# A two-layer hybrid decoder step on one core: split-weight ring restarted, first four output chunks of two stages done row by row, embedding gate moved to VectorE

## The reference

```python
for i in range(2):
    z = rmsnorm(h, norm1[i]) @ w_in[i]              # 2560 columns: pooling input, q, k, v, gate
    h = h + concat(pool(z), retention(z)) @ w_o[i]
    hn = rmsnorm(h, norm2[i])
    if i == 0:  f = (silu(hn @ wg) * (hn @ wu)) @ wd           # dense, D_FF = 2816
    else:       f = sum over 8 experts of gate_e * swiglu_e(hn)    # top 2 of 8, 1408 wide
    h = h + f
    gate = sigmoid(h @ w_ple_gate[i])
    h = h + gate * (p[i] @ w_ple[i])                # the embedding gate
y = rmsnorm(h, final_norm)
```

## Time and profile before

| | |
|---|---|
| median of three runs | 984.67 us |
| the profiled execution, its whole time | 982.37 us |
| its span, first to last instruction | 980.6 us |
| mean granted TensorE clock | 0.972 |
| TensorE busy | 925.4 us (94%) |
| VectorE busy | 718.1 us (73%) |
| ScalarE busy | 523.2 us (53%) |
| GpSimd busy | 141.7 us (14%) |
| share of the chain that ended last | PE 86%, DVE 5%, ACT 4%, issue 2%, POOL 2% |

### The profile page before, as it was taken

One profiled execution on the slowest core, in us unless ns is written; L12 is line 12 of the kernel. 1 busy time (PEld: TensorE's weight loads), 2 busy tenths in 40 slices (PEclk: granted clock), 3 DMA queues, 4 the chain that ended last, 5 costly groups with the idle time before them and its releaser, 6 DMA issues.

```text
span 980.6 us, 14780 instructions
## 1 busy us (share of the span) xinstructions
PE 925.4 (94%) x6081; PEld 808.2 (82%) x6081; DVE 718.1 (73%) x861; ACT 523.2 (53%) x578; POOL 141.7 (14%) x176
## 2 busy tenths in 40 slices
PE   3999999999999898999989999999999999999974
PEld 3999799999999797998867777777777777777773
DVE  3786476555656547785569888898898979898953
ACT  5322364443434345222438876777668667777442
POOL 3337121100110026425210000000000000000023
PEclk9999899999999999998989999999999999999987
DMA  9963356746764635634317997999789978999501
GB/s 322 306 220 98 83 174 195 196 142 194 199 191 144 200 130 141 213 102 110 123 61 257 403 338 247 390 351 373 284 320 361 351 283 324 375 335 406 182 2 45
DMA packets 119798, 224.85 MB, mean 229 GB/s; under 512 B 4882, under 2 KB 88978, under 8 KB 119584
## 3 DMA queue, kind: packets, MB, share of 16 engines
q1 hardware_dynamic: 117664, 216.63, 62.8%
q0 software_dynamic: 2064, 7.23, 3.2%
HBM read 220.31 MB, written 3.99 MB: 229 GB/s over the span
## 4 chain that ended last, share of the span: by engine, by line
PE 86%; DVE 5%; ACT 4%; issue 2%; POOL 2%; DMA 1%; SPq 0%; DVEq 0%; ACTq 0%; POOLq 0%
PE bank L683 13%; PE bank L684 13%; PE bank L685 13%; PE bank L932 8%; PE bank L930 8%; PE bank L931 8%; PE bank L952 4%; PE bank L954 4%; PE bank L953 4%; ACT whi L1098 2%; DVE wlo L1322 2%; PE bank L874 1%; PE bank L875 1%; PE bank L905 1%; POOL ssum L1792 1%
## 5 line engine op out<-in xcount | busy, mean ns | idle before, releaser
L1322 DVE TENSOR_TENSOR wlo<-raw,whi 128x1408 fp32r<-128x1408 f32 (+2 forms) x294 | 478.9, 1652 | 125.7 <-ACT whi L1098 125.5
L1098 ACT ACTIVATE whi<-raw 128x1408 fp32r<-128x1408 f32 (+2 forms) x294 | 397.1, 1380 | 192.1 <-PE bank L685 117.6
L683 PE MATMUL bank<-xh,whi 128*128 128x264 f32 x672 | 196.3, 292 | 15.7 <-DVE xl L1333 14.3
L684 PE MATMUL bank<-xl,whi 128*128 128x264 f32 x672 | 193.0, 287 | 0.0
L685 PE MATMUL bank<-xh,wlo 128*128 128x264 f32 x672 | 192.6, 287 | 0.0
L930 PE MATMUL bank<-whi,xeh 128*96 128x512 f32 (+1 forms) x384 | 143.6, 374 | 0.6 <-DVE hid L1610 0.6
L683 PEld LDWEIGHTS bank<-xh,whi 128*128 128x128 f32 x672 | 129.3, 192 | 17.7 <-DVE wlo L1322 10.8
L932 PE MATMUL bank<-whi,xel 128*96 128x512 f32 (+1 forms) x384 | 143.9, 375 | 0.0
L931 PE MATMUL bank<-wlo,xeh 128*96 128x512 f32 (+1 forms) x384 | 143.4, 373 | 0.0
L684 PEld LDWEIGHTS bank<-xl,whi 128*128 128x128 f32 x672 | 129.4, 193 | 0.3
L685 PEld LDWEIGHTS bank<-xh,wlo 128*128 128x128 f32 x672 | 128.6, 191 | 0.0
(11 more groups left out here) (225 smaller groups left out, 1344.8 us busy)
## 6 DMA issues: line engine op xcount, KB each, us to landing
raw<-in_moe_w_gate SPq DMA_DIRECT2D x32, 1408.0 KB, 7.3
raw<-in_moe_w_up SPq DMA_DIRECT2D x32, 1408.0 KB, 7.7
raw<-in_moe_w_down SPq DMA_DIRECT2D x40, 1024.0 KB, 6.9
raw<-in_w_in SPq DMA_DIRECT2D x20, 1024.0 KB, 8.4
raw<-in_ffn_w_down SPq DMA_DIRECT2D x16, 704.0 KB, 4.9
raw<-in_ffn_w_gate SPq DMA_DIRECT2D x10, 1024.0 KB, 5.4
raw<-in_ffn_w_up SPq DMA_DIRECT2D x10, 1024.0 KB, 5.5
raw<-in_w_o SPq DMA_DIRECT2D x8, 1024.0 KB, 7.1
```

The lines of the kernel that those rows point to most:

```text
L683: pe.matmul(out, w_hi, x_hi, start=start, stop=False)
L684: pe.matmul(out, w_hi, x_lo, start=False, stop=False)
L1098: act.activation(unit_hi(u), unit_raw(u), ACT.Copy).then_inc(hi_ready, 1)
L1322: dve.tensor_tensor(unit_lo(u), unit_raw(u), unit_hi(u).bitcast(F32), ALU.subtract).then_inc(lo_ready, 1)
```

## The change

Five edits.

1. `ring` takes an index at which it begins again at column 0: unit 46, the first of the last eight down units. The places of all later units change. For the units around the embedding gate of layer 0, `HIGH_LAST` (the unit that must have been used first) becomes: unit 55: 52 instead of 51; unit 56: 53 instead of 54; unit 57: 54 instead of 55; units 54, 58, 59 and 60 as before (50, 55, 56, 57). In the experts some units wait for one unit more, others for one less, and `SPLIT_AT` differs at 36 of its steps, each time by one step.
2. `four_chunks`: the first four output chunks (two units) of the feed-forward and of the second mixer are done as row blocks 0 to 5 of each of the four, then row blocks 6 and 7 of each. The norm's mean stands behind the third chunk's first six row blocks.
3. The multiplication by the gate is VectorE's, ahead of the addition.
4. ScalarE and VectorE finish one chunk after the other instead of by pairs.
5. In the last norm GpSimd adds six squares only; TensorE accumulates the last two itself, and a one-element root stands ahead of the last square.

```diff
-def ring(sizes, room):
+def ring(sizes, room, fresh=-1):
     at, taken, out = 0, [], []
-    for n in sizes:
-        if at + n > room:
+    for k, n in enumerate(sizes):
+        if at + n > room or k == fresh:
             at = 0
...
-HIGH_AT, HIGH_LAST = zip(*ring(COLS, HIGH_COLS))
+HIGH_AT, HIGH_LAST = zip(*ring(COLS, HIGH_COLS, U_FF[0] + PART_UNITS + 2 * GROUPS))
...
+            def four_chunks(u, n, before, norm):
+                for first_row, rows in ((0, 6), (6, 2)):
+                    for c in range(4):
+                        if first_row == 0:
+                            pe.wait_ge(lo_ready, u + c // 2 + 1)
+                            pe.wait_ge(acc_free, n + c - 3)
...
+                        for k in range(first_row, first_row + rows):
+                            if c == 0:
+                                pe.wait_ge(part_lo, before + k + 1)
+                            mm = weights_first(bank[(n + c) % 4][:, 0:T], H[:, k, own], L[:, k, own], xh[:, k, :], xl[:, k, :],
+                                               k == 0, k == DC - 1)
+                        if first_row:
+                            mm.then_inc(unit_used if c % 2 else acc_full, 1)
+                        elif c == 2:
+                            side_step(*norm)
...
             def feed_forward():
+                four_chunks(U_FF[0], A_FF[0], PARTS_AT[1], (0, "norm2"))
...
+                    if l == DEPTH:
+                        pe.wait_ge(ss_added, SQUARES_AT[6] + DC - 2)
+                        pe.matmul(b[:, 0:T], mean, ssum[:, :], start=True, stop=False)
+                        for m in (DC - 2, DC - 1):
+                            pe.wait_ge(sq_ready, SQUARES_AT[6] + m + 1)
+                            mm = pe.matmul(b[:, 0:T], mean, sq[:, m % 2, :], start=False, stop=(m == DC - 1))
...
+                if l:
+                    four_chunks(U_MIX[1], A_MIX[1], PARTS_AT[3], (1, "norm1"))
...
+            def finish_one(stage, m):
+                h_final(act, stage, m)
+                if stage in PARTS_AT:
+                    part(stage, m)
+                square(stage, m)
...
                         act.activation(sgp[:, m % 2, :], bank[n % 4][:, 0:T], ACT.Sigmoid).then_inc(gate_ready, 1)
-                    finish_pair(6 if l else 3, 2 * j)
+                        if l and m == DC - 1:
+                            act.activation(rstd[0:1, 0:1], rstd[0:1, 0:1], ACT.Sqrt)
+                        finish_one(6 if l else 3, m)
...
                     for m in (2 * j, 2 * j + 1):
+                        dve.wait_ge(gate_ready, DC * l + m + 1)
+                        dve.tensor_tensor(esb[l][:, m, :], esb[l][:, m, :], sgp[:, m % 2, :], ALU.mult).then_inc(ge_ready, 1)
                         dve.wait_ge(ge_ready, DC * l + m + 1)
                         add_h(None, m, esb[l][:, m, :])
-                    if l == 0:
-                        for m in (2 * j, 2 * j + 1):
+                        if l == 0:
                             finish(3, m)
...
-                for m in range(DC):
-                    pool.wait_ge(acc_free, A_PLE[l] + m + 1)
-                    pool.wait_ge(gate_ready, DC * l + m + 1)
-                    pool.tensor_tensor(esb[l][:, m, :], esb[l][:, m, :], sgp[:, m % 2, :], ALU.mult).then_inc(ge_ready, 1)
-                    if m % 2 and m > 1:
-                        add_square(6 if l else 3, m - 3)
-                        add_square(6 if l else 3, m - 2)
-                add_square(6 if l else 3, DC - 2)
-                add_square(6 if l else 3, DC - 1)
+                for m in range(DC - 2 * l):
+                    add_square(6 if l else 3, m)
```

More of the change, by code:

```diff
@@ L707, in unit_pair @@
                 chunk(n + 1, n + 1, u, DC, 256, 1, xhi, xlo).then_inc(unit_used, 1)
+            def four_chunks(u, n, before, norm):
[4 more added lines that the diff above has]
+                            pe.wait_ge(acc_free, n + c - 3)
+                        H = unit_hi(u + c // 2).rearrange("p (k w) -> p k w", k=DC)
+                        L = unit_lo(u + c // 2).rearrange("p (k w) -> p k w", k=DC)
+                        own = slice(c % 2 * P, (c % 2 + 1) * P)
+                        for k in range(first_row, first_row + rows):
[7 more added lines that the diff above has]
+                            side_step(*norm)
             def feed_forward():
+                four_chunks(U_FF[0], A_FF[0], PARTS_AT[1], (0, "norm2"))
                 for half in range(2):
@@ L712, in feed_forward @@
                     for i, (kind, _, w, a, _) in enumerate(PART):
+                        if i + half < 2 and half == 0:
+                            continue
                         pe.wait_ge(lo_ready, n.unit + (i + 1))
-                        row_ready = (f_lo, n.hidden) if i == 2 * GROUPS else (part_lo, PARTS_AT[1]) if i + half == 0 else None
+                        row_ready = (f_lo, n.hidden) if i == 2 * GROUPS else None
                         for m in range(w):
@@ L721, in feed_forward @@
                             mm.then_inc(acc_full if m < w - 1 else unit_used, 1)
-                        if i + half == 0:
-                            side_step(0, "norm2")
             def ple_chunks(l):
@@ L748, in side_step @@
                     pe.wait_ge(first_in, 16)
-                    pe.wait_ge(ss_added, SQUARES_AT[NORM_STAGE[l, name]] + DC)
-                    mm = pe.matmul(b[:, 0:T], mean, ssum[:, :], start=True, stop=True)
+                    if l == DEPTH:
[4 more added lines that the diff above has]
+                            mm = pe.matmul(b[:, 0:T], mean, sq[:, m % 2, :], start=False, stop=(m == DC - 1))
+                    else:
+                        pe.wait_ge(ss_added, SQUARES_AT[NORM_STAGE[l, name]] + DC)
+                        mm = pe.matmul(b[:, 0:T], mean, ssum[:, :], start=True, stop=True)
                 elif name[:2] in ("rq", "rk"):
@@ L1033, in _ @@
             for l in range(DEPTH):
+                if l:
+                    four_chunks(U_MIX[1], A_MIX[1], PARTS_AT[3], (1, "norm1"))
                 for j in range(10):
-                    unit_pair(U_MIX[l] + j, A_MIX[l] + 2 * j, xh, xl, (part_lo, PARTS_AT[3 * l]) if j == 0 else None)
+                    if l == 0 or j > 1:
+                        unit_pair(U_MIX[l] + j, A_MIX[l] + 2 * j, xh, xl, (part_lo, PARTS_AT[0]) if l + j == 0 else None)
                     for name in AFTER[j]:
-                        side_step(l, name)
+                        if (l, name) != (1, "norm1"):
+                            side_step(l, name)
                 side_step(l, "va")
```

## The result

The changed kernel takes 975.46 us (median of 4 runs, 975.08 to 977.73) against 984.55 us (983.88 to 984.93): ratio 0.9922 [0.9909, 0.9936], or 7.7 us less (6.3 to 9.0). The two medians themselves lie 9.1 us apart. Forecast: 975.2, -9.5. The two profiled executions lie closer together: 977.73 us with a span of 975.9, the slowest of its four, and 982.37 with 980.6, 2.2 us under its kernel's median. Their difference, -4.6 us, is what the two traces can explain.

The account below looks back on a forecast made before the run. TensorE, busy 94% of the span, was taken as the bound, leaving only its gaps. Terms -6.7 (gate through mixer's head), +1.4 (feed-forward's head), -4.2 (end) sum to -9.5: 984.67 to 975.2 us, range 971.5 to 980.0.

Parts of the forecast that it names:

- The ring: Layer 0 embedding gate: first product 4.22 us earlier, gap shrinking to 0.65 us, and 1.84 us more from full clock.
- rival E: Layer 0 gate: no earlier start because unit 56's raw data isn't there at 333.3; 981.2 us, chance 0.04.
- The gate's chain: Layer 0 gate, ScalarE and VectorE: 2.10 us per chunk, 0.35 lock-out at five places; `lo(60)` ends at 372.85.
- The mixer's head: Second mixer's first four chunks: TensorE idles 6.7 us for `lo(60)`, fourth chunk ends at 382.2; whole stretch gives 6.7 us.
- The feed-forward's head: Feed-forward's first four chunks: 2.0 us idle for `lo(15)`, a loss of 1.4 us, or 3.2 if the clock halves.
- The experts: Expert passages: ring places shift by up to one unit; no cost taken, 1.5 us either way as bound.
- rival D: Experts' ring: TensorE waits 1.38 us for two units at each of five passages, 13.8 us; 989.0 us, chance 0.04.
- The end: Last norm, sigmoid 7 to root: 4.2 us gained, between 3.8 and 4.4; root at 968.0 to 968.6 instead of 972.41.
- C: Both heads: new row order loses 2 us more each, later low parts holding chunk 3's first row; 979.2, chance 0.05.
- A: Gate and feed-forward: lock-outs cost 0.54 us at every chunk and the feed-forward's clock falls; 979.6 us, chance 0.13.
- B: Gate: GpSimd doesn't lock VectorE out at all; -11.5 us in sum, 973.2 us, chance 0.12.

Follow-up runs that it names:

- the run with the old order: Changed kernel without `four_chunks`, so the old row order at both the feed-forward's and the second mixer's head: 970.84 us, ratio 0.9877 to the kernel before.
- one-column sums: Changed kernel with GpSimd's seven additions of squares for the second mixer's norm replaced by one-column memsets (outputs wrong, time only): 977.6 us, ratio 0.993.
- the second measurement: The changed kernel itself, unaltered, run again beside the kernel before: 977.63 us, ratio 0.9938.
- row order and early unit 60 at the mixer: Changed kernel with old order at the feed-forward; at the second mixer new row order, unit 60's parts made before gate chunks 6 and 7: 971.44 us, ratio 0.9885.
- early low parts: Changed kernel with units 15 and 60's high and low parts made before the last two chunks at both layer 0 heads: 971.95 us, ratio 0.9874.
- ring begun twice: Changed kernel with old feed-forward order, unit 60 early at the mixer, and the ring begun anew also at expert 0's first down unit: 972.17 us, ratio 0.9882.

## Why the prediction came out as it did

- **The ring: right.** The gate's start was forecast at 338.65 in the time of before; 341.46 less the shift of 2.82 it arrived with is 338.64. The gap is 0.54 us and the clock full. By itself it gives 8.0 us, and rival E (data not there) is out.
- **The gate's chain: right.** `lo(60)` was to end at 372.85; 372.99 + 2.29 - 2.82 is 372.46. Four multiplications, not five, take 0.80 to 0.82 us; at the first place GpSimd has a copy of 0.41 us and no addition, which I overlooked. The price is 0.38 each, against 0.35. By the rule cited there (the Trainium skill, SBUF — State Buffer, "SBUF: two separate sides": whichever starts first has the port for its whole instruction) the multiplication of 364.11 would end 0.43 us behind GpSimd's addition. This trace agrees in direction, not in size: it ends at 364.92, 0.28 us behind it. The addition of 0.97 us in the earlier trace rows ends as early behind GpSimd's (0.29 us), so it doesn't bear out the whole lock-out either, as the prediction had it.
- **The mixer's head: right in kind, 1.1 us short.** Forecast gap 6.7, measured 6.00. From its end I counted 9.3 us to the fourth chunk's end; it took 10.7 (375.34 to 386.0, where the 60th product ends). Half clock lasted until 381.0 and cost 3.2 us, not the 1.84 read behind the gap of 4.77. So 5.6 us are won from unit 40 to 66 where I had 6.7. The row order's own price there was 2.8 us by the run with the old order, and I had charged 1.3.
- **The feed-forward's head: the term most out of size.** "A loss of 1.4 us. If a gap of 2.0 us already halves the clock ... it is 3.2." It was 3.1. The gap's end is nearly as forecast (145.27 for 145.5), its start isn't: TensorE reaches the head at 137.72 in place of 139.13 and is done with the 36 products at 142.31 in place of 143.47. The code up to there is the same in both kernels; between 120 and 140 us the granted clock was 1.00 in this execution and 0.91 in that of before. So TensorE idles 2.96 us, behind which the clock is 0.50. Four traces with this head (the changed kernel twice, without the ring's restart, one-column sums) show gaps of 2.95 to 2.97. In the fifth (multiplication on GpSimd) TensorE arrives at 138.71, the gap is 2.10, the clock stays up and the cost is 1.6. So mechanism right, size wrong: I took TensorE's arrival as fixed.
- **The experts: the other mis-sized term.** Forecast 0 with 1.5 either way, measured +1.6: rival D's mechanism at a tenth of its price. The 3.0 us in hand at unit 144 were read at one passage and don't cover the others; TensorE pays some 0.28 us per expert.
- **The end: right.** -4.2 forecast; sigmoid to root 3.08 us in place of 7.36 is -4.3, and sigmoid 7 itself ran as TensorE paced it. What I didn't say is that this term needs edits 3 and 4 too. The table load stands 1.29 us ahead of the next operation (965.11 to 966.40). The Trainium skill (ScalarE: Activation LUTs, "What ACT_TABLE_LOAD costs") puts a switch of tables at 2.66 us, about half of it a drain. The load's 1.28 us agree with its figure for the load alone; a drain is again not what this trace shows. (From its figure I had put the gain at 2.9 us; 4.2 less the difference of 1.37 is 2.8.)
- **Sum.** Traced, in order of time: -0.3 (ahead of the feed-forward) + 3.1 (its head) - 5.6 (the mixer's head) + 0.1 + 1.6 (the experts) + 0.7 (from there to sigmoid 7, not forecast; the granted clock between 920 and 940 us is 0.85 in place of 0.92) - 4.2 (the end) = -4.6 us; forecast -9.5. The median came out at 975.46 all the same, since the profiled execution of before is 2.2 us fast for its kernel and that of after 2.3 us slow; against the second measurement (-6.1 us) the forecast is 3.4 us too good. The forecast's nearness to 975.46 is partly luck.
- **Rivals.** C (row order dearer than charged, 979.2) was nearer the truth in its place than the 0.05 I gave it, with another cause: not a later low part but an earlier TensorE, and the half clock. A's feed-forward half came true (3.2), its lock-outs at all eight chunks didn't. B is out.

## What to carry over

Ask for each operand of the first products of a stage which of them is made last, and order the consumer so that all work not needing it stands ahead; changing only one side's order cost 6 to 9 us here. When a buffer ring is begun anew to free one place, count the waits at every later passage too. And price a stall from both ends: the engine that waits may arrive earlier than it did.

## What the runs showed of the hardware

The length of a gap alone doesn't tell whether the products behind it run at half clock (1.2 GHz). At half clock the rows take 0.42 us at a pace of 0.22, at full clock 0.28 at 0.12. Behind gaps of 2.71 and 2.96 us the clock fell, and so it did behind one of 1.82 with a second of 1.53 soon after. Gaps near 2 us went either way. Full clock followed one of 2.01 (row order and early unit 60 at the mixer) and one of 2.10 (multiplication on GpSimd):

```profile
367.05 0.36 PE L683 MATMUL bank<-xh,whi 128*128 128x264 f32 x1 [2.01 <-DVE h L1534]
...
369.18 0.29 PE L685 MATMUL bank<-xh,wlo 128*128 128x264 f32 x1
```

Half clock came within 1.3 us of the end of one of 1.99 (early low parts), one of 1.98 (ring begun twice) and one of 2.00 (the mixer's head with the multiplication on GpSimd). In the trace of before the clock was also at half between 122 and 124 us, where the longest gap in the ten microseconds ahead is 0.2 us. So what TensorE did in the microseconds around a gap matters besides it; which rule sets it isn't settled here. And a small lead won in mid-program doesn't always keep: twice (one-column sums, old order at the feed-forward only) 2 to 3 us of it didn't reach the end, part of it lost to half clock in later stages whose code was the same.
